# Two-layer attention and expert trunk: both query rotations and all head roots on GpSimd, new order between the latent projections and attention one

## The reference

```python
c_q = rms_norm(h @ w_dq, g_cq)
q = (c_q @ w_uq).reshape(B, S, MLA_HEADS, MLA_QK)            # 16 heads of 96
kv = (c_kv @ w_ukv).reshape(B, S, MLA_HEADS, MLA_NOPE + MLA_V)
k = jnp.concatenate([k_nope, k_pe], axis=-1)
q = rms_norm(q, g_qn)        # x * rsqrt(mean(x*x) + EPS) * gain, per head
k = rms_norm(k, g_kn)
q = jnp.concatenate([q[..., :MLA_NOPE], rope(q[..., MLA_NOPE:], pos)], axis=-1)
k = jnp.concatenate([k[..., :MLA_NOPE], rope(k[..., MLA_NOPE:], pos)], axis=-1)
o = block_causal_attention(q, k, v, MLA_QK ** -0.5)
```

## Time and profile before

| what | value |
|---|---|
| median of 3 runs (lowest, highest) | 1520.61 us (1520.49, 1523.8) |
| the profiled execution, its own time | 1523.13 us |
| its span | 1521.3 us |
| mean granted TensorE clock | 0.977 |
| busy: TensorE, VectorE, ScalarE, GpSimd | 1451.0, 1148.2, 954.7, 42.7 us |

### The profile page before, as it was taken

The page is one execution under the profiler, slowest core; times in us unless marked ns, Lnnn a source line. Parts: engine busy times, 40 slices in busy tenths (PEclk is TensorE's granted clock), DMA queues, the critical chain, the costliest instruction groups (busy, mean ns, idle before and its releaser), DMA issues.

```text
span 1521.3 us, 20025 instructions
## 1 busy us (share of the span) xinstructions
PE 1451.0 (95%) x7249; PEld 1217.4 (80%) x7249; DVE 1148.2 (75%) x1049; ACT 954.7 (63%) x918; POOL 42.7 (3%) x79
## 2 busy tenths in 40 slices
PE   5788999998987899999999999999999999999998
PEld 5577999997876688878878878888887887887886
DVE  4665544546674889879888888888987998888894
ACT  4455433444563677767777777687776767677772
POOL 3120000000100000000000000000000000000000
PEclk9889999998999899999999999999999999999999
DMA  8145455554532599989989999998998998999992
GB/s 303 57 122 167 138 181 181 192 188 140 185 123 86 195 337 376 372 305 375 383 320 353 375 332 331 390 360 306 379 378 326 342 382 328 339 384 332 336 376 89
DMA packets 150625, 424.67 MB, mean 279 GB/s; under 512 B 11149, under 2 KB 41018, under 8 KB 150586
## 3 DMA queue, kind: packets, MB, share of 16 engines
q1 hardware_dynamic: 146752, 420.39, 76.0%
q10 hardware_dynamic: 3450, 3.69, 0.8%
q0 software_dynamic: 384, 0.07, 0.1%
HBM read 423.08 MB, written 4.19 MB: 281 GB/s over the span
## 4 chain that ended last, share of the span: by engine, by line
PE 93%; DVE 4%; ACT 1%; issue 1%; POOL 0%; DMA 0%; ACTq 0%; POOLq 0%; SPq 0%; DVEq 0%
PE ps L1370 82%; PE ps L1365 4%; PE ps L1693 2%; PE ps L1667 2%; PE ps L1484 2%; PE ps L1504 1%; DVE wl_a L919 1%; ACT wh_a L596 0%; DMA xr<-in_x 0%; ACT tn L605 0%; DVE kT L1047 0%; DVE bias L1062 0%; DVE xr L955 0%; PE ps L1645 0%; DVE htl L938 0%
## 5 line engine op out<-in xcount | busy, mean ns | idle before, releaser
L919 DVE TENSOR_TENSOR wl_a<-raw,wh_a 128x2048 fp32r<-128x2048 f32 (+1 forms) x230 | 516.0, 2270 | 123.1 <-ACT wh_a L596 123.1
L596 ACT ACTIVATE wh_a<-raw 128x2048 fp32r<-128x2048 f32 (+1 forms) x230 | 434.1, 1906 | 209.6 <-PE ps L1370 200.3
L919 DVE TENSOR_TENSOR wl_b<-raw,wh_b 128x2048 fp32r<-128x2048 f32 x168 | 378.8, 2286 | 35.4 <-ACT wh_b L596 34.3
L596 ACT ACTIVATE wh_b<-raw 128x2048 fp32r<-128x2048 f32 x168 | 319.3, 1925 | 56.5 <-PE ps L1370 53.3
L1370 PE MATMUL ps<-wh_a,hth 128*128 128x512 f32 (+2 forms) x576 | 226.3, 393 | 5.6 <-DVE htl L938 3.5
L1370 PE MATMUL ps<-wl_a,hth 128*128 128x512 f32 (+2 forms) x576 | 223.4, 388 | 0.0
L1370 PE MATMUL ps<-wh_a,htl 128*128 128x512 f32 (+2 forms) x576 | 223.4, 388 | 0.0
L1370 PE MATMUL ps<-wh_b,hth 128*128 128x512 f32 x448 | 178.4, 398 | 0.0
L1370 PE MATMUL ps<-wh_b,htl 128*128 128x512 f32 x448 | 174.6, 390 | 0.0
L1370 PE MATMUL ps<-wl_b,hth 128*128 128x512 f32 x448 | 174.4, 389 | 0.0
L1370 PEld LDWEIGHTS ps<-wh_a,hth 128*128 128x128 f32 x576 | 109.3, 190 | 30.1 <-issue 6.7
(11 more groups left out here) (230 smaller groups left out, 2050.9 us busy)
## 6 DMA issues: line engine op xcount, KB each, us to landing
raw<-in_moe_w SPq DMA_DIRECT2D x336, 1024.0 KB, 7.3
raw<-in_ffn_w SPq DMA_DIRECT2D x33, 1024.0 KB, 5.3
raw<-in_a_w_o SPq DMA_DIRECT2D x4, 1024.0 KB, 5.7
raw<-in_b_w_q SPq DMA_DIRECT2D x4, 1024.0 KB, 5.1
raw<-in_kv_w_k SPq DMA_DIRECT2D x4, 1024.0 KB, 5.1
raw<-in_kv_w_v SPq DMA_DIRECT2D x4, 1024.0 KB, 5.0
raw<-in_b_w_o SPq DMA_DIRECT2D x4, 1024.0 KB, 5.2
bias<-bias_wide ACTq DMA_DIRECT2D x8, 384.0 KB, 3.2
```

The lines of the kernel that those rows point to most:

```text
L596: nc.scalar.activation(dst[:, 0:w], raw[:, n % RAW, 0:w], ACT.Copy).then_inc(hi_done, 1)
L919: nc.vector.tensor_tensor(l[:, 0:w], raw[:, n % RAW, 0:w], h[:, 0:w].bitcast(fp32), ALU.subtract).then_inc(lo_done, 1)
```

## The change

The power on GpSimd takes the place of the Sqrt, the reciprocal and the Newton step. In layer 0 it is made in two parts of 32 columns: the queries' roots (`rsq_done`) behind the rotations, and the keys' roots (`rs_done`) when their sums are there. In layer 1 it is one power on 64 columns, behind the norms, and VectorE waits for it in step g = 5 instead of g = 3. GpSimd rotates both halves of the queries, each when its squares are made. ScalarE makes `hi(9)` and the queries' squares ahead of the seventh piece's copy, VectorE makes `lo(9)` ahead of the eighth's. The buffer `rtmp` and two pairs of semaphores go. In the diff VectorE's `attention` stands ahead of the loop only because its text was moved.

```diff
@@ GpSimd
-            pool.wait_ge(sq_done[0], 2)
-            chain(rotate(nc.gpsimd, 1))
-            nc.gpsimd.tensor_tensor(q_rope(1), roptmp[:, 1, 0], roptmp[:, 1, 1], ALU.add).then_inc(rq_done, 1)
+            for t in range(T):
+                pool.wait_ge(sq_done[0], t + 1)
+                chain(rotate(nc.gpsimd, t))
+                nc.gpsimd.tensor_tensor(q_rope(t), roptmp[:, t, 0], roptmp[:, t, 1], ALU.add).then_inc(rq_done, 1)
+
+            def head_roots(parts, n):
+
+                r, v = (x[:, parts].rearrange("p a t h -> p (a t h)") for x in (rsh, ssh))
+                chain(nc.gpsimd.tensor_scalar(v, v, 1.0 / n, EPS, ALU.mult, ALU.add))
+                return nc.gpsimd.tensor_tensor(r, v, negh[:, 0:1].to_broadcast([P, v.shape[1]]), ALU.pow)
+
+            pool.wait_ge(sh_done[0], T)
+            head_roots(slice(0, 1), QK).then_inc(rsq_done, 1)
+            pool.wait_ge(sh_done[0], 4 * T)
+            head_roots(slice(1, 2), QK).then_inc(rs_done[0], 1)
...
             norm(2)
+            pool.wait_ge(sh_done[1], 2 * T)
+            head_roots(slice(0, 2), HD).then_inc(rs_done[1], 1)
             pool.wait_ge(rs_done[1], 1)
             attention(1)
@@ ScalarE
-                if i in (1, 3, 5, 9):
-                    hi({1: 6, 3: 7, 5: 8, 9: 9}[i])
-                if i == 6:
+                if i in (1, 3, 5):
+                    hi({1: 6, 3: 7, 5: 8}[i])
+                if i == 5:
+                    hi(9)
...
-            def head_std(la):
-                act.wait_ge(var_done[la], 1)
-                nc.scalar.activation(rsh[:].rearrange("p a t h -> p (a t h)"), ssh[:].rearrange("p a t h -> p (a t h)"),
-                                     ACT.Sqrt).then_inc(std_done[la], 1)
-
-            head_std(0)
...
-                if g == 3:
-                    head_std(1)
@@ VectorE
-                if i == 9:
-
-                    dve.wait_ge(sq_done[0], 1)
-                    dve.wait_ge(rope_tab, 2)
-                    chain(rotate(nc.vector, 0))
-                    nc.vector.tensor_tensor(q_rope(0), roptmp[:, 0, 0], roptmp[:, 0, 1], ALU.add).then_inc(rq_done, 1)
-                if i in (1, 3, 5, 9):
-                    lo({1: 6, 3: 7, 5: 8, 9: 9}[i])
-                if i in (7, 11):
+                if i in (1, 3, 5, 6):
+                    lo({1: 6, 3: 7, 5: 8, 6: 9}[i])
+                if i in (7, 9):
...
-                last = nc.vector.tensor_scalar(ssh[:, 1, t, :], ssh[:, 1, t, :], ss[:, 4 + t:5 + t], None, ALU.add)
-            chain(last)
-
-            def head_roots(la, n):
-
-                r, v = (a.rearrange("p a t h -> p (a t h)") for a in (rsh[:], ssh[:]))
-                nc.vector.tensor_scalar(v, v, 1.0 / n, EPS, ALU.mult, ALU.add).then_inc(var_done[la], 1)
-                dve.wait_ge(std_done[la], 1)
-                chain(nc.vector.reciprocal(r, r))
-                chain(nc.vector.tensor_tensor(rtmp[:], v, r, ALU.mult))
-                chain(nc.vector.tensor_tensor(rtmp[:], rtmp[:], r, ALU.mult))
-                chain(nc.vector.tensor_scalar(rtmp[:], rtmp[:], -0.5, 1.5, ALU.mult, ALU.add))
-                nc.vector.tensor_tensor(r, r, rtmp[:], ALU.mult).then_inc(rs_done[la], 1)
-
-            head_roots(0, QK)
...
+                nc.vector.tensor_scalar(ssh[:, 1, t, :], ssh[:, 1, t, :], ss[:, 4 + t:5 + t], None, ALU.add).then_inc(sh_done[0], 1)
             dve.wait_ge(rq_done, 2)
-            dve.wait_ge(rope_tab, 2)
+            dve.wait_ge(rsq_done, 1)
             for _ in attention(0):
                 pass
...
                 if g == 5:
 
                     att1 = attention(1)
+                    dve.wait_ge(rs_done[1], 1)
                     next(att1)
...
-                if g == 3:
-                    dve.wait_ge(sh_done[1], 4)
-                    head_roots(1, HD)
-                    dve.wait_ge(rs_done[1], 1)
```

More of the change, by code:

```diff
@@ L152, in trunk_kernel @@
         rsh = sb("rsh", [P, 2, T, HEADS])
-        rtmp = sb("rtmp", [P, 2 * T * HEADS])
         nmax = sb("nmax", [P, 2, T, 2])
@@ L281, in trunk_kernel @@
         sh_done = [sem("sh_done0"), sem("sh_done1")]
-        var_done = [sem("var_done0"), sem("var_done1")]
-        std_done = [sem("std_done0"), sem("std_done1")]
         zeroed = sem("zeroed")
@@ L287, in trunk_kernel @@
         rq_done = sem("rq_done")
+        rsq_done = sem("rsq_done")
         rk_done = sem("rk_done")
@@ L1113, in attention, with k_sums @@
                 yield
-            dve.wait_ge(rs_done[0], 1)
+            for i in range(14):
+                if i % 2 == 1:
+                    dve.wait_ge(unit_used, latent_out(i)[0])
+                    nc.vector.tensor_copy(latent_out(i)[1], ps[4 + i % 4][:, :]).then_inc(pj_v[0], 1)
+                if i in (1, 3, 5, 6):
+                    lo({1: 6, 3: 7, 5: 8, 6: 9}[i])
+                if i in (7, 9):
+                    t = i // 2 - 3
+                    dve.wait_ge(sq_done[0], t + 1)
+                    nc.vector.reduce_sum(ssh[:, 0, t, :], squares[:, t * HEADS * QK:(t + 1) * HEADS * QK].rearrange("p (h w) -> p h w", w=QK),
+                                         AX).then_inc(sh_done[0], 1)
+            def k_sums(h):
+                for t in range(T):
+                    at = (2 * t + h) * HEADS * NOPE // 2
+                    dve.wait_ge(sq_done[0], T + 2 * h + t + 1)
+                    nc.vector.reduce_sum(ssh[:, 1, t, h * HEADS // 2:(h + 1) * HEADS // 2],
+                                         squares[:, at:at + HEADS * NOPE // 2].rearrange("p (h w) -> p h w", w=NOPE),
+                                         AX).then_inc(sh_done[0], 1)
+            k_sums(0)
+            k_sums(1)
+            dve.wait_ge(kps_done, 2)
+            for t in range(T):
+                dve.wait_ge(sh_done[0], 3 * T)
+                nc.vector.tensor_scalar(ssh[:, 1, t, :], ssh[:, 1, t, :], ss[:, 4 + t:5 + t], None, ALU.add).then_inc(sh_done[0], 1)
             dve.wait_ge(rq_done, 2)
-            dve.wait_ge(rope_tab, 2)
+            dve.wait_ge(rsq_done, 1)
             for _ in attention(0):
```

## The result

| kernel | median | lowest to highest | runs |
|---|---|---|---|
| before | 1521.83 us | 1520.49 to 1523.8 | 6 |
| the change | 1527.76 us | 1527.12 to 1528.35 | 6 |

The ratio of the change to before is 1.0039, 95% interval 1.0027 to 1.0051, so 4.1 to 7.8 us slower; the medians differ by 5.9. The forecast was 9.5 us more, 1530.1; the time is in the range, and on the likeliest side. One execution of the kernel before, among those that experiments e5 to e8 are compared with, took 2106.41 us at a mean granted clock of 0.651 and is left out of every figure.

The account below looks back on a forecast made before the run. TensorE, busy 95% of the span, was taken as the bound, so only its waits count: +1.2 us in layer 0 and +8.3 in layer 1 gave +9.5, 1520.6 to 1530.1 us, range 1514.3 to 1532.5.

Parts of the forecast that it names:

- The price of a power: GpSimd's roots in both layers: each further column costs 0.163 us, so 5.6 us for 32 columns and 10.8 for 64.
- Rivals A: GpSimd's powers are cheap per column, below 0.045 us; keys' transposes come 6.0 us earlier, time 1514.6; chance 0.18.
- B: GpSimd's powers cost 0.05 to 0.12 us per column; time 1518.2 at 0.08, between 1516 and 1525; chance 0.22.
- Place one: TensorE's wait from latent projections to attention one in layer 0: keys' transposes start at 82.6 instead of 81.39, +1.2 us.
- the lock: GpSimd and two-input VectorE instructions in SBUF exclude each other for the whole instruction, taken to include a power's full length.
- Place two: Layer 1 projections: the 64-column power delays VectorE's subtractions, TensorE waits 7.0 or 5.5 us and its clock drops, +8.3 us.
- The clock term: Layer 1, behind TensorE's long wait: granted clock falls to 0.50, giving away about 2.2 us.
- Rival C: Full price per column but no lock while a power computes: +0.3 in layer 0, +0.5 in layer 1, 1521.4; chance 0.13.

Follow-up runs that it names:

- e5: The change, with layer 1's power meant to start ahead of VectorE's subtraction (it did not); 1527.46 us, 1.0036 of the kernel before.
- e8: The change, with VectorE's subtraction of unit 12 made ahead of its wait for layer 1's roots; 1527.32 us, 1.0034 of the kernel before.
- e4: The change, with layer 1's power split into two of 32 columns, queries' early and keys' later; 1524.22 us, 1.0012 of the kernel before.
- e9: The change, with VectorE delayed by a wait and four small memsets so layer 1's power surely starts first; 1523.85 us, 1.0008 of the kernel before.
- e2: The kernel before, with only layer 1's roots made by one 64-column power on GpSimd; 1524.84 us, 1.0022 of the kernel before.

## Why the prediction was right, and which steps were not

**The price of a power: right.** Columns and times are 1 at 0.551, 32 at 5.43, 64 at 10.53: (5.43 - 0.551)/31 = 0.157 us a column, (10.53 - 5.43)/32 = 0.159. The forecast was 0.163, 5.6 and 10.8. The price is linear, and the two-column row was enough to find it. Rivals A and B needed under 0.12 and are out. The Trainium skill's GPSIMD Engine Reference (section 3.1) gives some 2.6 cycles per element for a tensor_tensor, and the measurement beside it is of an add. The estimate of 0.14 us for 64 columns from it stands against 10.5 here, so it does not hold for a power.

**Place one: right in mechanism, a little over in size.** Forecast +1.2 us at the keys' transposes, measured 82.23 against 81.39, +0.84, and 0.3 of this was there before TensorE's first latent matmul (39.56 against 39.24). In the gap alone it is +0.5. The step that was over is the lock again: the forecast let VectorE's first `qn` in ahead of the second power and kept the second `qn` out until that power's end, which put 0.5 us in front of `kn`. Here the first `qn` began at 75.24 and cost the power 0.2 us (5.60 against 5.43); the second ended at 76.35, inside the power, and `kn` followed the power at once (81.20). The restart at 62.05 (forecast 61.85), the end of the sums at 72.4 (72.1), and the two powers (to 74.7 and 81.1; measured 75.14 and 81.12) came as worked out.

**Place two: the step on the lock failed.** "It holds the lock until 403.9 + 10.8" was wrong. What the runs show instead: the power waits out a VectorE subtraction with two inputs in SBUF that began ahead of it (12.67 us against 10.53), but a subtraction that begins behind it waits 0.08 us (e4) or not at all (e9). The Trainium skill's rule (SBUF — State Buffer, Who interferes with whom) that the lock is held for the full instruction agrees with the multiplies of the earlier trace rows and not with the power, beside which a subtraction of 2.29 us takes 2.29. So unit eleven's subtraction was not late, and TensorE waited 1.53 us at the transposes (417.65, forecast 420.8) and 0.60 at the first score.

**The clock term there was wrong too.** Of the 8.3 us, 2.2 were for a clock at half behind a long wait. The wait was short, and from 410 to 425 us the granted clock stayed at 1.00. It fell later, at the end of attention two:

```profile
460.00:462.00 2.00, 1.41 (x9) 1.28 (x8) 0.42 (x1) 0.38 (x1) 0.00 (x0) 0.72 0.00 0
462.00:464.00 2.00, 2.00 (x12) 2.00 (x11) 0.00 (x0) 0.65 (x3) 0.00 (x0) 0.50 0.00 0
```

Before, both windows are at 1.00. This drop is inside the 0.4 us behind the first score, and so inside the 3.0 us that layer 1 lost in place of 8.3.

**Rival C** (full price, no lock) was thus the right mechanism for layer 1, with a chance of 0.13, and mis-sized: it had the power end at 414.7, TensorE just in time, and +0.5. It left out that a subtraction that slips in ahead lengthens the power by 2.14 us, nearly its whole 2.29, and that `qn` in front of two subtractions makes `kT` late. e9, where the power does start first, is rival C: 1.0008 of before, 1.2 us (0 to 2.6), against the +0.8 of that rival.

So the forecast of slower held for part of its reasons: the price stood, of the 9.5 us the 1.2 became 0.8 and the 8.3 became 3.0 in the profiles. That the time still fell near the forecast is in part luck, since the step that carried most of it, VectorE shut out for the length of a power, was wrong.

## What to carry to other kernels

Take the price of an operation per column from the smallest shapes in the trace before moving it to another engine: a power on GpSimd is 0.16 us a column here, so it suits one or two columns and not 32 or 64, unless something as long runs beside it. Test the parts of a change apart: here a new order worth 5 us was hidden under powers that cost 11. Of two long operations in one queue, here only the first had the cover, and the second stood on the path whole. And before reading a stage's length as the worth of an edit, compare the granted clock over that stage: in e8 it made 2.2 of 2.5 us.

## What the runs showed of the hardware

- GpSimd's power and VectorE's subtraction hold each other up in one direction. A power of 64 columns issued 0.01 us after a subtraction takes 12.67 us for 10.53; a subtraction issued 0.01 us after a power of 32 columns takes 2.37 for 2.29, and others inside a power 2.29.
- Which of the two starts first decided 3.9 us between the medians (e9, where the power began 0.54 us ahead of the subtraction, against the change, where it began 0.01 us behind).
- The clock drop at the end of attention two (between 456 and 466 us, to 0.50) stood in the profiles of the change, e2, e5 and e8, all with the 64-column power started late, and in no other; e9 has the same power, started first, and no drop.
- TensorE's clock at the end of attention one fell in eight of the thirteen profiles (from 1.00 to 0.60 to 0.77 in the lowest window of 4 us between 116 and 128 us), among them one of two kernels with the same code up to there.
- Behind the norm ahead of layer 1 the clock was back at 0.98 to 1.00 some 6 us after the norm's start in e2 and e8, and some 12 us after it in the other eleven profiles; layer 1's sums came 2.2 us earlier for it.
